# Feed-forward over six PSUM banks, and another deal of the context stream's steps beside the first block

## Chip, cores and metric

The kernel runs on one core of one Trainium2 chip. The metric is device time in microseconds of that core, from one launch that takes all inputs from HBM and writes the output there. A profile of one execution stands beside the timed ones.

## What is computed

Two models run one after the other on 256 tokens of 1024 channels, all in fp32. The first (`first_block`) has two layers, each a hybrid mixer (an SSD branch of 4 groups with 8 heads each, and a retention branch of 4 heads) and a SwiGLU feed-forward. The second (`second_block`) has two layers of latent attention, a Fourier branch and a pooling branch, and after them 128 experts per token, which are rows of two tables picked by top-k. Beside its tokens it carries a context of 256 rows through layer 0, which does not depend on the first model.

```python
def first_block(x, ...):
    for l in range(2):
        h = h + hybrid_mixer(rmsnorm(h, norm_mix_w[l]), ...)
        h = h + swiglu(rmsnorm(h, norm_ffn_w[l]), w_gate_up[l], w_down[l])

def second_block(x, c, ctx, ...):
    for l in range(2):
        last = l == 1
        m_x, m_c = _modulation(c, ...), _modulation(c_ctx, ...)
        hc = _modulate(ctx, norm1_g[l], m_c[0], m_c[1])
        if last: kv_c = _ctx_keys_values(hc, lp)
        else: mix_c, kv_c = _token_mix(hc, lp, None, None)
        mix_x, _ = _token_mix(h, lp, ang, kv_c)
        x = x + m_x[2] * mix_x
        x = x + m_x[5] * _peer(h2, w_pq[l], peer_keys[l], peer_down[l], peer_up[l])
        if not last:
            ctx = ctx + m_c[2] * mix_c
            ctx = ctx + m_c[5] * _peer(hc2, ...)
    return _rmsnorm(x, final_g)
```

`_peer` scores keys, ranks them twice for each of 8 heads, and takes for every token 128 rows of `peer_down` (a dot product with the token) and 128 rows of `peer_up` (a weighted sum).

## The kernel before

The program is a list of items (`put(kind, ...)`); each of the five engines walks the list in its order and does its own part of every item, so the list is the order on PE, DVE (VectorE), ACT (ScalarE), POOL (GpSimd) and SP (SyncE) alike. An engine does what stands next and waits there if its input is not ready.

Two generators make the list. `x_stream` (here the x stream) runs the first model, then the second on x. `context_stream` runs the second model's modulation (48 `mod` items), the context's mixing of layer 0 (attention, Fourier, pooling, gates, `mix`, `token_out`), its queries and ranking, and its experts: 512 steps, each a `fetch` (an indirect DMA of one row for each of 128 tokens, 512 KB, issued by POOL) with a `down` (DVE line 2179) or an `up` (DVE line 2190). The rows come in a ring of nine places.

`streams` deals the two: every `yield` of the x stream adds its number (7 by default) to a clock `ta`, every `yield` of the context stream adds its own to `tb` (1.5 for an expert step), and the context stream moves while `tb <= ta * pace`. `PACES` holds the pace of the modulation, of the mixing, of queries and ranking, and of the experts. When the first model is at its end it yields `"alone"`: what is left of the context stream is put into the list there, ahead of everything that the x stream does in the second model:

```python
            elif step == "alone":
                for _ in live.pop("b", ()):
                    pass
```

A weight chunk is 1 MB, loaded by SP in list order into a ring of slots (three for the mixer of the first model, five for its feed-forward, two for the context). A chunk's products fill one PSUM bank (`Use`, `Banks`), and the bank comes free when DVE or ACT has read it. The mixer uses two banks for chunks (`pa`), two for turns and sums (`pa2`), two for heads and outputs (`py`), and the context two (`pb`). In the feed-forward 22 chunks (`ffn_in`, read by ACT and then by DVE lines 1911 and 1913) go over `wide`, four banks, and then 8 `ffn_out` and 2 `ffn_last` items fill four banks with sums. `ffn_out` number 0 waits until DVE has finished `ffn_in` number 21.

In the SSD branch each of the groups g has `conv_in`, `conv_in`, `gate_in`, `gate_in` of the next group, with four `heads` items between them (PE line 1429 writes the decay logs, ACT lines 2308 to 2314 and DVE lines 1840 and 1841 make the weights, PE lines 1419 to 1421 sum with them), the turn of the group before (`group_end`) and `group_gate`.

## Time and profile before

| | |
|---|---|
| median of 3 runs | 4160.32 us (4160.32 to 4169.17) |
| the profiled execution | 4172.86 us, span of its instructions 4171.6 us |
| PE, DVE, POOL busy | 3669.1 us, 2321.4 us, 1283.5 us |
| DMA | 1208.65 MB, 290 GB/s over the span |

Times in rows count from the first instruction. The profile's L numbers are lines of the kernel before. The first model's two layers take the span's first half, to 2164.8 us, the context stream ends just before that, and the rest is the second model on x. "Idle before" is the time an engine stood still ahead of a group of instructions, and "<-" names what it waited for. PE clk is the granted clock of TensorE as a share of full speed.

### The profile page before, as it was taken

Reading aid. Unit: us, or ns where it says so; the run is one execution under the profiler, and the core shown is the slowest. Engines: PE = TensorE matmul, PEld = TensorE weight load, DVE = VectorE, ACT = ScalarE, POOL = GpSimd, SP = SyncE. Lnnn points to the kernel's source line nnn. Section 1 sums busy time; section 2 is a strip of 40 time slices with the busy share of each in tenths; the row PEclk is TensorE's granted clock in tenths of the full one; section 3 lists DMA queues with packets and bytes.
Section 4 is the critical chain, followed back from the end, with each engine's and each line's share of the span. In section 5 each row is a group of like instructions: output and inputs, shape, how many; then the busy total and the mean of one; then the engine's idle time right before and its main releaser. Section 6 shows DMA issues by size and latency. Waiting matters only on the chain. (4 is left out here: it accounts for less than half of the span.)

```text
span 4171.6 us, 41042 instructions
## 1 busy us (share of the span) xinstructions
PE 3669.1 (88%) x14584; PEld 2587.9 (62%) x14584; DVE 2321.4 (56%) x5464; ACT 657.2 (16%) x1800; POOL 1283.5 (31%) x1125
## 2 busy tenths in 40 slices
PE   8988999998998889999998988777878898877777
PEld 6667788887856778888746874333335786433333
DVE  3432011557767887766751156766763126777875
ACT  2332001110001320100002211111112211111111
POOL 1100000000655566665620013433441002344443
PEclk9999999999999999999999999888999999998889
DMA  8742344334998889998963359988996327999998
GB/s 319 282 194 90 123 151 182 121 129 148 410 396 306 291 327 402 405 383 351 413 250 115 106 223 357 407 344 365 416 414 269 109 106 296 380 420 420 417 419 332
DMA packets 207818, 1208.65 MB, mean 290 GB/s; under 512 B 23696, under 2 KB 24848, under 8 KB 96000
## 3 DMA queue, kind: packets, MB, share of 16 engines
q0 software_dynamic: 154368, 855.71, 51.3%
q1 hardware_dynamic: 53248, 350.32, 22.1%
q8 instruction: 118, 1.93, 0.2%
q14 instruction: 84, 0.69, 0.0%
HBM read 1204.79 MB, written 1.15 MB: 289 GB/s over the span
## 5 line engine op out<-in xcount | busy, mean ns | idle before, releaser
L1308 PE MATMUL bank<-big 128*128 128x256 f32 (+5 forms) x9848 | 2141.4, 378 | 59.8 <-issue 8.7
L1308 PEld LDWEIGHTS bank<-big 128*128 128x128 f32 (+2 forms) x9848 | 1833.9, 191 | 373.6 <-issue 68.0
L2499 POOL DMA_INDIRECT big<-in_pboth,big x1024 | 1219.9, 1191 | 1229.2 <-PE bank L1695 734.8
L1695 PE MATMUL bank<-big 128*128 128x512 f32 x2048 | 1006.0, 650 | 273.5 <-ACT big L2463 273.5
L2179 DVE CUSTOM_DVE_ANT_0 big<-big 128x1024 f32<-128x1024 f32 x768 | 927.5, 1224 | 322.1 <-DMA big<-in_pboth,big 305.4
L1695 PEld LDWEIGHTS bank<-big 128*128 128x128 f32 x2048 | 415.3, 208 | 855.3 <-issue 497.4
L2486 POOL TENSOR_TENSOR big<-big 128x1 f32<-128x1 f32 (+1 forms) x49 | 37.7, 769 | 1502.2 <-DVE big L1749 1502.2
L2190 DVE SCALAR_TENSOR_TENSOR big<-big 128x1024 f32<-128x1024 f32 x254 | 326.3, 1284 | 60.6 <-DMA big<-in_pboth,big 36.6
L2463 ACT ACTIVATE big<-big 128x128 f32<-128x128 f32 x512 | 164.7, 391 | 241.9 <-DVE big L2158 237.0
L1343 PE MATMUL bank<-big 128*128 128x128 f32 x596 | 95.5, 296 | 64.0 <-ACT big L2310 20.6
L2453 ACT ACTIVATE big<-big 128x4 f32<-128x4 f32 (+2 forms) x134 | 27.7, 207 | 725.2 <-DVE big L2154 718.4
L1498 PE MATMUL bank<-big 128*128 128x512 f32 x256 | 114.3, 609 | 19.4 <-DVE big L1913 19.4
L2035 DVE TENSOR_REDUCE big<-bank 128x1 f32<-128x512 f32 (+1 forms) x48 | 28.9, 603 | 173.6 <-PE bank L1596 173.6
L1343 PEld LDWEIGHTS bank<-big 128*128 128x128 f32 x596 | 75.0, 154 | 81.4 <-issue 35.0
L1822 DVE SCALAR_TENSOR_TENSOR big<-big,bank 128x512 f32<-128x512 f32 x32 | 22.0, 688 | 146.2 <-ACT big L2291 143.9
L1498 PEld LDWEIGHTS bank<-big 128*128 128x128 f32 x256 | 49.7, 195 | 83.2 <-issue 63.0
L1899 DVE SCALAR_TENSOR_TENSOR big<-big,bank 128x256 f32<-128x256 f32 x32 | 13.5, 421 | 151.5 <-PE bank L1308 151.4
L1806 DVE SCALAR_TENSOR_TENSOR big<-bank,big 128x255 f32<-128x255 f32 (+1 forms) x144 | 62.7, 478 | 61.6 <-ACT big L2279 59.9
L2248 ACT ACTIVATE big<-big 128x1024 f32<-128x1024 f32 x26 | 27.4, 1055 | 423.8 <-DVE big L1919 160.4
L2057 DVE SCALAR_TENSOR_TENSOR big<-big,bank 128x512 f32<-128x512 f32 x36 | 24.8, 689 | 103.6 <-PE bank L1308 103.6
L2431 ACT ACTIVATE big<-bank,big 128x256 f32<-128x256 f32 x72 | 30.2, 471 | 281.3 <-PE bank L1308 281.3
L2492 POOL DMA_DIRECT2D big<-in_wmod x48 | 25.8, 540 | 152.3 <-PE bank L1520 152.3
(203 smaller groups left out, 2178.5 us busy)
## 6 DMA issues: line engine op xcount, KB each, us to landing
big<-in_w SPq DMA_DIRECT2D x104, 1024.0 KB
big<-in_wmod POOLq DMA_DIRECT2D x48, 1024.0 KB, 8.6
big<-in_wgu SPq DMA_DIRECT2D x44, 1024.0 KB
big<-in_wzg SPq DMA_DIRECT2D x36, 1024.0 KB, 4.8
big<-in_wro SPq DMA_DIRECT2D x32, 1024.0 KB
big<-in_wpq SPq DMA_DIRECT2D x24, 1024.0 KB, 7.0
big<-in_wd SPq DMA_DIRECT2D x22, 1024.0 KB
big<-in_pboth,big POOLq DMA_INDIRECT x1024, 10.1
```

Source lines behind the costliest of these rows:

```text
L1308: last = pe.matmul(o, a, b, start=(i == 0), stop=(i == n - 1))
L1343: last = pe.transpose(o[:, i, :], b, ident)
L1498: last = pe.matmul(us[2 * tt + n].ap, act[:, 2 * i + k, tt * P:tt * P + P], wk[:, k, 512 * n:512 * n + 512], start=(i + k == 0), stop=False)
L1695: last = pe.matmul(u.ap, d.ap, row[:, 512 * i:512 * i + 512], start=(k == 0), stop=(k == 127))
L1806: i = v.scalar_tensor_tensor(c[:, m, s:256], o[:, m, 0:256 - s], conv["w"][m][:, 3 - s:4 - s], c[:, m, s:256], ALU.mult, ALU.add)
L2035: step(v.reduce_max(sm[:, c:c + 1], u.ap[:, 0:nk * P], AX.X))
L2179: v.tensor_tensor_reduce(row, row, h, 1.0, 0.0, ALU.mult, ALU.add, out).then_inc(done[0], 1)
L2190: v.scalar_tensor_tensor(at, s.ap, by, at, ALU.mult, ALU.add).then_inc(done[0], 1)
L2431: last = e.activation(sc.ap[:, m, :], by2(u.ap)[:, m, :], ACT.Tanh, scale=0.5, bias=bias[m])
L2463: s.activation(d.ap, p.ident, ACT.Copy, scale=by).then_inc(diag[0], 1)
L2486: g.tensor_tensor(r.sm[:, 8 + r.at:8 + r.at + r.n], r.sm[:, 4 + r.at:4 + r.at + r.n], r.sm[:, 12:13].to_broadcast([P, r.n]), ALU.pow).then ...
L2499: g.indirect_dma_start(out=s.ap, out_offset=None, in_=table, in_offset=bass.IndirectOffsetOnAxis(ap=index, axis=0)).then_inc(s.full[0], 16)
```

## The change

Five edits, all in the planner. `PACES` of the context: mixing 1.8 to 3.0, queries and ranking 1.1 to 0.9, experts 0.72 to 0.66. Numbers behind `yield` in the SSD branch: in layer 0 of the x stream (`l == 0`) nearly as before, in layer 1 small where DVE has much to do and larger elsewhere. The order inside a group: the turn of the group before stands ahead of a `heads` item instead of behind it, and `dt_sums` and the first `group_mask` come after two of the four first inputs. The last four retention outputs have no context steps between them. The feed-forward has six banks (`six`), and each `ffn_out` waits only for the two activations that it reads.

```diff
@@ -126,7 +126,7 @@
         self.before, self.ss, self.var, self.done = before, ss, var, done
 
 
-PACES = (0.8, 1.8, 1.1, 0.72)
+PACES = (0.8, 3.0, 0.9, 0.66)
 A_SIZE = 27648
 BIG_N = 53208
 SIDE = 8300
@@ -367,7 +367,7 @@
                 w, u = chunk()
                 BC.append(conv(u, 2 * i, qk[:, 2 * i:2 * i + 2, :], None))
                 put("conv_in", ws=[w], hT=hT, conv=BC[i], ready=None if i else hT_ok)
-                yield
+                yield 4 if l else 7
             BC_ok = BC[3]["done"]
             if l == 0:
                 put("block_consts", rmask=rmask, rope=rope)
@@ -514,10 +514,14 @@
                 yield 2
 
             gots = [{"turn": []} for _ in range(8)]
-            yield from group_inputs(0, gots[0])
+            inputs = group_inputs(0, gots[0])
+            for _ in range(2):
+                next(inputs)
+                yield 4 if l else 7
             dts_ok = tick("dt_summed")
             put("dt_sums", u=self.pa2.take(), dts=dts, ready=la_ok, done=dts_ok)
             group_mask(0)
+            yield from inputs
             pairs = group_heads(0, gots[0])
             next(pairs)
             for g in range(4):
@@ -525,13 +529,19 @@
                 end = group_end(g - 1, gots[g - 1]) if g else iter(())
                 for i in range(4):
                     next(nxt)
-                    yield 5.8
+                    if l == 0:
+                        yield 5.8
+                    elif i != 1:
+                        yield 7 if i else 3.5
+                    if i == 1:
+                        next(end, None)
                     next(pairs)
+                    if i == 0:
+                        next(end, None)
                     if i == 2 and g < 3:
                         group_mask(g + 1, gots[g]["cb_read"])
                     if i < 3:
-                        next(end, None)
-                        yield 5.8
+                        yield 6 if i < 2 else 5
                 next(nxt, None)
                 group_gate(g, gots[g])
                 yield 2.5
@@ -568,7 +578,7 @@
                             c.free(self.mt_ok)
                         put("branch_out", ws=[w], u=u, YT=YT, ready=y_ok if n == 0 else [], sig=s.ap[:, m, :], s_ok=s_ok,
                             MT=MT[:, n, :], c=c, done=self.mt_ok)
-                        yield 7.2 if first or n < 6 else 1
+                        yield 7.2 if first or n < 4 else 1
                     s.free(u.free)
 
             yield from merge(True, y_ok, group_end(3, gots[3]))
@@ -609,31 +619,32 @@
             yield 27
 
             fr = Ring([wa[2], wt[0], wt[1], wa[0], wa[1]])
+            six, acts = Banks(self.pa.banks + self.pa2.banks + self.py.banks), []
             for i in range(22):
-                w, u, c = self.load(fr, t["wgu"][l, i], 2048), wide.take(), tmp.take()
+                w, u, c = self.load(fr, t["wgu"][l, i], 2048), six.take(), tmp.take()
                 w.free(u.full)
                 c.free(u.free)
                 put("ffn_in", ws=[w], u=u, hT=hT, c=c, dst=area[:, i, :], tanh=tick("ffn_tanh"),
                     ready=None if i else hT_ok)
-                act_ok = u.free
+                acts.append(u.free)
                 yield
             if l:
                 fw_ok = tick("d_fnorm", 16)
                 put("load_row", dst=fw, src=t["fnorm"][0].to_broadcast([P, 1024]), done=fw_ok, before=[self.x_ok])
-            us = [wide.take() for _ in range(4)]
+            us = [six.take() for _ in range(4)]
             for i in range(8):
                 w = self.load(fr, t["wd"][l, i], 2048)
                 done = tick("ffn_part")
                 w.free(done)
-                put("ffn_out", ws=[w], us=us, act=area, i=i, ready=None if i else act_ok, done=done)
+                put("ffn_out", ws=[w], us=us, act=area, i=i, ready=acts[2 * i + 1], done=done)
                 yield
             ws = [self.load(fr, t["wd"][l, i], 2048) for i in range(8, 11)]
-            put("ffn_last", ws=ws, three=ws, us=us[0:2], act=area, tt=0)
+            put("ffn_last", ws=ws, three=ws, us=us[0:2], act=area, tt=0, ready=acts[17::2])
             put("ffn_add", us=us[0:2], X=X[:, 0, :])
             self.x_ok0 = us[1].free
             r0 = stats(0, late)
             yield 10
-            put("ffn_last", three=ws, us=us[2:4], act=area, tt=1)
+            put("ffn_last", three=ws, us=us[2:4], act=area, tt=1, ready=acts[17::2])
             for w in ws:
                 w.free(us[3].full)
             if l == 0:
@@ -1487,8 +1498,8 @@
 
     def ffn_out(ws, us, act, i, ready, done):
         wk = by2(ws[0].dst)
-        if ready:
-            pe.wait_ge(*ready)
+        pe.wait_ge(*ready)
+        if i == 0:
             for u in us:
                 opened(u)
         pe.wait_ge(*ws[0].full)
@@ -1499,9 +1510,10 @@
                                      start=(i + k == 0), stop=False)
         last.then_inc(done[0], 1)
 
-    def ffn_last(three, us, act, tt, **_):
+    def ffn_last(three, us, act, tt, ready, **_):
         for i, w in enumerate(three):
             wk = by2(w.dst)
+            pe.wait_ge(*ready[i])
             pe.wait_ge(*w.full)
             for k in range(2):
                 for n, u in enumerate(us):
```

In the item list the 512 expert steps are dealt anew. Steps of the context's experts per stretch of the x stream, before and after: feed-forward of layer 0 with its outputs 112 and 103; layer 1 until its first `heads` 31 and 20; its groups up to `branch_gate` 88 and 70; the SSD outputs 44 and 40; retention 78 and 72; retention outputs and `mix_out` 59 and 49; feed-forward with its outputs 100 and 97; behind the last instruction of the first model 0 and 61, of which 4 stand ahead of `"alone"` and 57 are dealt there.

The first place is DVE's queue at the end of the first model. L1919/L1931 is `ffn_add` (before/after), L1924/L1936 `full_norm`, its last work there; L2190/L2202 is `up`, L2209/L2221 and L2212/L2224 `peer_add`, and L1749/L1761 with L1982/L1994 the first norm of the second model. Before:

```order
1835 L2190 SCALAR_TENSOR_TENSOR big<-big 128x1024 x29
1836 L2209 TENSOR_TENSOR big<-big 128x1024 x2
1837 L2212 TENSOR_TENSOR big<-big 128x1024 x2
1838 L1919 SCALAR_TENSOR_TENSOR big<-bank,big 128x512 x2
...
1844 L1924 SCALAR_TENSOR_TENSOR big<-big 128x1024
1845 L1749 TENSOR_SCALAR big<-big 128x1
1846 L1982 TENSOR_SCALAR big<-big 128x1024
```

After:

```order
1820 L2202 SCALAR_TENSOR_TENSOR big<-big 128x1024 x27
1821 L1931 SCALAR_TENSOR_TENSOR big<-bank,big 128x512 x2
...
1828 L1936 SCALAR_TENSOR_TENSOR big<-big 128x1024
1829 L2202 SCALAR_TENSOR_TENSOR big<-big 128x1024 x61
1830 L2221 TENSOR_TENSOR big<-big 128x1024 x2
1831 L2224 TENSOR_TENSOR big<-big 128x1024 x2
1832 L1761 TENSOR_SCALAR big<-big 128x1
1833 L1994 TENSOR_SCALAR big<-big 128x1024
```

The expert steps ended ahead of the first model's last sums; now 61 of them and the context's sum stand between its last instruction and the second model's first.

The second place is DVE's queue in layer 1, group 1, from `heads` to `heads` (L1806/L1818 and L1815/L1827 are `conv_in`, L1862/L1874 the turn of the group before). Before:

```order
1340 L2190 SCALAR_TENSOR_TENSOR big<-big 128x1024 x3
1341 L1840 SCALAR_TENSOR_TENSOR big<-big 128x256
...
1345 L2190 SCALAR_TENSOR_TENSOR big<-big 128x1024 x3
1346 L1806 SCALAR_TENSOR_TENSOR big<-bank,big 128x255 x2
...
1349 L1815 SCALAR_TENSOR_TENSOR big<-big 128x512
1350 L2190 SCALAR_TENSOR_TENSOR big<-big 128x1024 x3
1351 L1840 SCALAR_TENSOR_TENSOR big<-big 128x256
...
1355 L1862 TENSOR_TENSOR big<-bank,big 128x4x128 x2
```

After:

```order
1287 L2202 SCALAR_TENSOR_TENSOR big<-big 128x1024
1288 L1852 SCALAR_TENSOR_TENSOR big<-big 128x256
...
1292 L2202 SCALAR_TENSOR_TENSOR big<-big 128x1024 x3
1293 L1818 SCALAR_TENSOR_TENSOR big<-bank,big 128x255 x2
...
1296 L1827 SCALAR_TENSOR_TENSOR big<-big 128x512
1297 L1874 TENSOR_TENSOR big<-bank,big 128x4x128 x2
1298 L1852 SCALAR_TENSOR_TENSOR big<-big 128x256
```

No expert step stands any more between a `conv_in` and the `heads` behind it, and one instead of three ahead of the first `heads`.

The third place is SP's queue where the context goes from its mixing to its queries, in layer 0. `in_iota` and `in_keys` wait for the context's last `token_out` (the load of `in_wout` is its weight); `in_w` and `in_wro` are chunks of the x stream. Before:

```order
76 L2517 DMA big<-in_wout 128x2048 x3
77 L2517 DMA big<-in_w 128x2048
78 L2562 DMA big<-in_iota 128x16
79 L2566 DMA big<-in_keys 128x2048
80 L2517 DMA big<-in_w 128x2048 x2
```

After:

```order
66 L2529 DMA big<-in_wout 128x2048 x2
67 L2574 DMA big<-in_iota 128x16
68 L2578 DMA big<-in_keys 128x2048
69 L2529 DMA big<-in_wro 128x2048
```

A chunk of the x stream stood between the last weight and the wait; now the next chunk of the x stream is behind it.

## Rows read from the trace of the kernel before

**Rows 1.** The page: busy time, share of the span and instructions of each engine.

```profile
PE 3669.1 (88%) x14584; PEld 2587.9 (62%) x14584; DVE 2321.4 (56%) x5464; ACT 657.2 (16%) x1800; POOL 1283.5 (31%) x1125
```

**Rows 2.** Stretches of the first model: start and end, length, busy times, clock, DMA.

```profile
core 0: us, PE busy (x) PEld busy (x) DVE busy (x) ACT busy (x) POOL busy (x), PEclk, DMA share, GB/s
...
857.30:1009.50 152.20, 140.89 (x651) 120.61 (x649) 105.82 (x398) 12.61 (x24) 1.82 (x3) 0.98 0.37 132
1009.50:1182.00 172.50, 154.79 (x704) 134.19 (x705) 125.79 (x281) 8.54 (x23) 100.42 (x80) 0.96 0.90 358
...
1269.10:1396.20 127.10, 110.42 (x527) 96.62 (x527) 105.63 (x189) 27.68 (x71) 67.43 (x52) 0.89 0.83 300
1396.20:1547.00 150.80, 125.86 (x675) 110.89 (x674) 133.87 (x183) 50.71 (x142) 91.02 (x71) 0.92 0.87 318
1547.00:1790.20 243.20, 238.86 (x1101) 205.27 (x1101) 181.17 (x288) 18.38 (x39) 163.10 (x128) 0.99 1.01 401
1790.20:1924.20 134.00, 125.93 (x572) 106.37 (x570) 74.03 (x121) 10.22 (x18) 69.03 (x54) 0.97 0.93 360
1924.20:2087.20 163.00, 152.76 (x704) 132.99 (x704) 122.90 (x129) 8.45 (x22) 112.92 (x84) 0.98 0.99 398
```

**Rows 3.** DVE in order of time, end of the first model: start, length, line, idle before.

```profile
2086.90 16.89 DVE L2190 SCALAR_TENSOR_TENSOR big<-big 128x1024 f32<-128x1024 f32 x12
...
2136.84 2.36 DVE L2209 TENSOR_TENSOR big<-big 128x1024 f32<-128x1024 f32 x2 [4.74 <-DMA big<-mods]
2139.24 2.36 DVE L2212 TENSOR_TENSOR big<-big 128x1024 f32<-128x1024 f32 x2
...
2167.72 1.29 DVE L1924 SCALAR_TENSOR_TENSOR big<-big 128x1024 f32<-128x1024 f32 x1 [0.74 <-POOL big L2486]
2171.49 0.15 DVE L1749 TENSOR_SCALAR big<-big 128x1 f32<-128x1 f32 x1 [2.49 <-DMA big<-in_cs]
```

**Rows 4.** PE in order of time: the second model's first chunk.

```profile
2176.88 7.43 PE L1308 MATMUL bank<-big 128*128 128x128 f32 x35 [1.74 <-DVE big L1989]
```

**Rows 5.** PE in order of time, both feed-forwards: three idle spells.

```profile
1046.11 10.23 PE L1308 MATMUL bank<-big 128*128 128x256 f32 x38 [8.55 <-DVE big L1913]
...
1182.01 2.90 PE L1498 MATMUL bank<-big 128*128 128x512 f32 x3 [9.12 <-DVE big L1913]
...
2087.24 10.99 PE L1498 MATMUL bank<-big 128*128 128x512 f32 x21 [10.28 <-DVE big L1913]
```

**Rows 6.** DVE in order of time: the first expert step.

```profile
1044.03 1.23 DVE L2179 CUSTOM_DVE_ANT_0 big<-big 128x1024 f32<-128x1024 f32 x1 [8.12 <-DMA big<-in_pboth,big]
```

**Rows 7.** PE in order of time: the first mix_out of layer 0.

```profile
970.37 4.89 PE L1308 MATMUL bank<-big 128*128 128x256 f32 x12 [5.36 <-issue]
```

**Rows 8.** PE's waits, 1396.2 to 1547 us: line, for whom, us, times, longest.

```profile
PE bank L1343 <- ACT big L2310: 15.2, 3, 6.6
PE bank L1419 <- DVE big L1841: 9.8, 5, 2.7
```

**Rows 9.** Groups of DVE instructions, 1396.2 to 1547 us: busy us, mean ns.

```profile
L2190 DVE SCALAR_TENSOR_TENSOR big<-big 128x1024 f32<-128x1024 f32 x67 | 86.0, 1284 | 5.9 <-issue 0.4
```

**Rows 10.** SP, then PE, in order of time: the modulation's end.

```profile
272.02 1.14 SPq L2540 DMA_DIRECT2D mods<-big  x4
274.20 0.36 SPq L2517 DMA_DIRECT2D big<-in_w  x1
...
272.13 1.09 PE L1343 MATMUL bank<-big 128*128 128x128 f32 x4 [3.18 <-DVE big L1942]
...
282.45 1.94 PE L1343 MATMUL bank<-big 128*128 128x128 f32 x8 [4.96 <-ACT big L2265]
```

**Rows 11.** SP, then PE, in order of time: the context's last token_out.

```profile
704.95 0.91 SPq L2517 DMA_DIRECT2D big<-in_w  x2
...
712.05 4.14 PE L1308 MATMUL bank<-big 128*128 128x256 f32 x11 [2.56 <-DMA big<-in_w]
```

**Rows 12.** PE in order of time, the context's mixing: an attention step, a gate.

```profile
381.35 0.41 PE L1343 MATMUL bank<-big 128*128 128x128 f32 x2 [1.13 <-ACT big L2412]
...
492.92 67.35 PE L1308 MATMUL bank<-big 128*128 128x256 f32 x302 [2.93 <-DMA big<-in_wzg]
```

## Prediction

> **What bounds the kernel now.** I read the page's busy shares first, then the stretches, then the idle spells of PE and DVE inside them. PE is busy for 3669 of 4171.6 us [rows 1], so the end moves only where PE gains or loses idle time or clock. By stretches [rows 2] the first model has three regimes. In the SSD outputs and the retention (1547 to 1790 us) PE is busy for 238.9 of 243.2 us: nothing to gain. In the feed-forwards PE misses 17.7 of 172.5 us and 10.2 of 163.0, nearly all of it in spells of 8.55, 9.12 and 10.28 us that wait for DVE [rows 5]. In layer 1 from 1269 to 1547 us PE is busy for 236 of 278 us at a clock of 0.89 and 0.92, while DVE is busy for 240: DVE's expert steps set the pace there. The context stream ends just ahead of the second model, so a step dealt earlier costs or saves nothing by itself; a step left at the end would have DVE alone.
>
> **The bill at the end.** 61 `up` steps now stand on DVE between `full_norm` and the second model's first norm, which feeds PE's first chunk. Twelve in a run took 16.89 us, 1.41 each [rows 3]: 61 x 1.41 = 85.8 us. Behind them the wait of `peer_add` for the modulation's row (4.74) and its two instructions (2 x 2.36) make 9.5 [rows 3], and the first chunk follows the norm by 2176.88 - 2171.49 = 5.4 [rows 3, 4]. Today the whole way from the end of `full_norm` (2169.0) to that chunk is 7.9. So the end pays 85.8 + 9.5 + 5.4 - 7.9 = **92.8**. Bounds: at 1.284 a step, the mean among other work [rows 9], the steps take 78.3, and if the row of the modulation is there early 4.7 go: 80.6. If each step took a tenth more: 101. A fetch moves 0.524 MB; at 401 GB/s [rows 2] that is 1.31 us, so DMA doesn't make it longer than DVE.
>
> **What the first model gives back.**
> - Feed-forward of layer 0. The 8.55 us come when a chunk finds none of four banks free, since DVE reached its `ffn_in` behind the ranking and a first expert step that waited 8.12 for its rows [rows 6]; six banks let PE run two chunks (some 14 us) further. The 9.12 come because `ffn_out` 0 waits for activation 21, now for activation 1. The same matmuls take 152.8 busy in layer 1 and 154.8 here at the lower clock; I take 153.8, so 172.5 becomes 153.8: **-18.7**, and about 2 (that difference of clock) behind the second spell: **-2.1**.
> - The end of layer 0's mixer (857 to 1009.5): 11.3 idle, 5.36 of it ahead of the first `mix_out` [rows 2, 7]. With no context steps between the last four outputs DVE makes that input early, and fewer ranks stand there: **-8.3**; bounds 0 and 11.3.
> - Layer 1 until group 1 (127.1 us, DVE 105.6): 50 steps become 35, that is 31 to 20 and 19 to 15. 15 steps at 1.33, about midway between 1.284 and 1.41, are **-20**. PE's 110.4 at 0.89 are about 100 at full clock, so the floor is not met.
> - Groups 1 to 3 (150.8, DVE 133.9, 67 steps [rows 9]): 12 fewer x 1.284 = 15.4. PE waits 15.2 us for ACT's line 2310 and 9.8 for DVE's 1841 [rows 8]; the first has other causes (the order of ACT), so I take **-12**. Bounds: 0, and PE alone at full clock, 125.9 x 0.92 = 116 to 118, a gain of 33.
> - 1547 to 1790: 4.3 idle [rows 2], **-3**. Then to 1924: 8.1 idle, with ten steps fewer **-2**, since the norm's chain stands there in any case.
> - Feed-forward of layer 1: the spell of 10.28 and its clock, **-11**.
>
> Together **-77.1**.
>
> **A rule against the move.** In layer 1 from 1547 us on the steps now lie under PE work: PE 98%, DVE 74%, DMA 1.01 [rows 2]; before that DVE was the limit. The Trainium skill ("Perfetto Trace Analysis", Optimization Strategy) says that a kernel with several regimes may gain by interleaving them; the change does the reverse for the steps at the end. This case's trace agrees for the retention and not for the groups. By the rule alone (rival E) the time would be 4239, by the rows 4194.
>
> **What layer 0 loses by the faster mixing.** Mixing steps move ahead of where they stood, so PE meets more of them in a row, each with a chain of its own.
> - The modulation's end: PE waits 3.18 and 4.96 there [rows 10], with x chunks between. SP's store of the modulation (272.02) had an x chunk's load behind it; now the load of the values' weight stands behind that wait, and `low_rank` directly behind the turn that feeds it: one more such wait, the mean of a longer one and clock, **+5.8** (bounds 0 and 9).
> - Attention: a step right behind another waited 1.13 for ACT [rows 12]; four or five more of them in runs, and two more in keys and values: **+7**. Against that the gate's load wait of 2.93 and its clock go, as the gates now stand further apart from the load of their first weight: **-4.1** [rows 12]. Bounds of the two together: -4 and +12.
> - The end of the mixing: `in_iota` and `in_keys` wait on SP for the last `token_out`. An x chunk's load stood ahead of them and the chunk's wait was 2.56 [rows 11]; now the next x chunk is queued behind. From issue to use was 712.05 - 704.95 = 7.1; with the two loads of keys ahead about 9.4, so +6.8, and 2.2 of clock: **+9** (bounds 0 and 12).
>
> Together **+17.7**.
>
> **Sum.** 92.8 - 77.1 + 17.7 = +33.4. The profiled execution has a span of 4171.6 (its time 4172.9), 12 above the median of the runs, 4160.3, which is the lowest of them too; the difference carries to the median: 4160.3 + 33.4 = **4194**. The measurement can tell about 0.3%, 12.5 us, from no change.
>
> **Rivals.**
> - A, the forecast, own range 4178 to 4208 (the bill's bounds are -12 and +8, those of layer 0's losses -22 and +6, and they don't all fall together): **0.49**.
> - B, payback in full and no new waits: in layer 0 the mixing steps hide behind x chunks (17.7 back), groups 1 to 3 give 15.4 and not 12, and retention's end 7 and not 2: 4194 - 17.7 - 8.4 = 4168, with bounds 4160 to 4173. For it: the losses rest on queue order, of which no row shows the new form. Against: the SP queue's wait is certain, only its length isn't. **0.20**.
> - C, the other side, faster: layer 1's groups and inputs become bound by PE alone. Then 277.9 falls to 100 + 117 = 217, a gain of 61 in place of 32, and with B's layer 0: 4194 - 29 - 17.7 = 4147. It decides once the gains less losses pass 92.8 + 12.5 = 105. For it: DVE's load falls by a fifth there and six yields move steps away from `heads`. Against: PE's 15.2 us for ACT don't depend on them. **0.11**.
> - D, the feed-forward keeps its length: its DMA share is 0.90 and 0.99 (358 and 398 GB/s [rows 2]), so with PE's spells gone the chunks come late instead. About 30 of the 18.7 + 2.1 + 11 is missing: 4194 + 30 = 4224. Against: layer 0 has room for 401 GB/s, 172.5 x 358/401 = 154, and both have fewer fetches. Half of it, in layer 1, gives 4204, still A. **0.15** for over 4208.
> - E, no step that is taken out of layer 1 or the mixer's end gives anything back, since PE would wait there for ACT or its own sums: 20 + 12 + 8.3 + 3 + 2 = 45 are missing, 4239. For it: the 15.2 us for ACT [rows 8]. Against: DVE's 133.9 of 150.8 and 105.6 of 127.1 us, with PE below full clock because it stands still. **0.05**.
>
> **Numbers.** The range from 4163 to 4221 takes in A, most of B and over half of D. Faster by over 0.3% is C, 0.11; within 0.3% is B, 0.20; slower is A, D and E, 0.69.
>
> **What would show it.** In the profile after: PE idle for about 105 us between `ffn_last` and the first chunk of the second model (12 today: 2164.8 to 2176.9), DVE's line 2202 x61 at 1.41 each, and line 2221 behind it with a wait for `mods` of about 5. No spell of 8 to 10 us in either feed-forward. Layer 1 to the end of group 3 some 246 us in place of 278. The first model's last PE work near 2165 - 59 = 2106. In layer 0 an idle spell of about 9 us that ends with the load of an `in_wro` chunk after the last `token_out`, and a wait of PE for the values' weight at the modulation's end. Wrong would make it: steps at the end at 1.28 or less or a modulation's row that is loaded ahead (toward B), PE bound groups (C), a DMA share at 1.0 in the feed-forwards with PE waiting for `wgu` or `wd` (D).

## The result, and the profile after

The changed kernel takes 4233.36 us (median of 4 runs, 4227.09 to 4244.06), beside 4163.78 us for the kernel before on the same chip: the ratio is 1.0167, with a 95% interval of 1.0145 to 1.0188. It is slower by some 70 us, where +33 was forecast, and lies above the range.

The page of the changed kernel, busy times; it answers to [rows 1]:

```profile
PE 3648.2 (86%) x14584; PEld 2573.9 (61%) x14584; DVE 2324.1 (55%) x5464; ACT 658.4 (16%) x1800; POOL 1284.0 (30%) x1125
```

The stretches of the changed kernel, cut at the same places of the program as those of [rows 2]. The first one is all up to the first feed-forward, the last two are the way from the matmuls that stand behind the first model's last sums to the second model's first chunk, and the second model from there on:

```profile
core 0: us, PE busy (x) PEld busy (x) DVE busy (x) ACT busy (x) POOL busy (x), PEclk, DMA share, GB/s
0.00:1036.00 1036.00, 947.17 (x4684) 771.46 (x4684) 360.50 (x1073) 175.49 (x441) 37.38 (x70) 0.96 0.46 171
1036.00:1188.60 152.60, 152.59 (x704) 133.22 (x705) 104.65 (x215) 8.26 (x22) 89.92 (x74) 1.00 0.94 378
1275.30:1382.90 107.60, 100.92 (x526) 88.73 (x527) 84.85 (x182) 28.11 (x71) 45.07 (x37) 1.00 0.80 279
1382.90:1527.10 144.20, 124.05 (x674) 110.81 (x674) 117.86 (x170) 50.81 (x142) 72.50 (x57) 0.93 0.77 281
1527.10:1772.80 245.70, 238.75 (x1101) 205.19 (x1101) 173.53 (x230) 18.29 (x39) 149.09 (x119) 0.99 0.98 380
1772.80:1903.10 130.30, 123.32 (x572) 105.29 (x570) 61.02 (x113) 10.03 (x17) 57.12 (x45) 1.00 0.86 328
1903.10:2055.70 152.60, 152.60 (x704) 133.19 (x705) 111.80 (x166) 8.26 (x22) 101.01 (x77) 1.00 0.98 394
...
2133.50:2238.40 104.90, 9.25 (x36) 7.31 (x37) 88.59 (x78) 6.35 (x13) 61.25 (x55) 0.54 0.87 322
2238.40:4225.80 1987.40, 1639.82 (x5202) 945.71 (x5202) 1130.96 (x3125) 345.13 (x1021) 584.95 (x527) 0.94 0.77 311
```

Read from the top, this is the account, forecast first. Up to the first feed-forward +17.7 - 8.3 = +9.4, measured 1036.0 - 1009.5 = **+26.5**. First feed-forward 172.5 to 152.6, forecast -18.7, measured -19.9; what stands behind it -2.1 and -0.4. Layer 1 until group 1: -20 and -19.5. Groups 1 to 3: -12 and **-6.6**. Until 1790 us: -3 and **+2.5**. The mixer's end: -2 and -3.7. Last feed-forward with its outputs: -11 and -12.3. So the first model's last sums end 33.4 us earlier (2164.9 to 2131.5). The matmuls behind them wait for `ffn_add`, which in the changed kernel stands behind expert steps:

```profile
2133.48 6.27 PE L1364 MATMUL bank<-big 128*128 128x256 f32 x20 [1.94 <-DVE big L1931]
```

The forecast counts the bill from the end of DVE's `full_norm`. That comes 31.6 us earlier (2169.0 to 2137.4), not 59.4, and from there to the second model's first chunk it is 101.0 us instead of 7.9: +93.1, where 92.8 was forecast. The first chunk comes 2238.4 - 2176.9 = 61.5 us later. From there on the program is the same in both kernels, and took 1994.7 us in the profile before and 1987.4 in this one.

### The profile page after: what moved, and what is told of

Its sections match the earlier page's. It is cut to its first block and busy times, and to the rows that moved or that the text cites. A ratio compares the mean times of both kernels' runs of the same rounds, so it can differ in the third digit from the quotient of the medians.

```text
span 4225.8 us, 41067 instructions
## 1 busy us (share of the span) xinstructions
PE 3648.2 (86%) x14584; PEld 2573.9 (61%) x14584; DVE 2324.1 (55%) x5464; ACT 658.4 (16%) x1800; POOL 1284.0 (30%) x1125
## 5 line engine op out<-in xcount | busy, mean ns | idle before, releaser
L1319 PE MATMUL bank<-big 128*128 128x256 f32 (+4 forms) x9848 | 2134.2, 377 | 50.4 <-DMA big<-in_wro 9.5
L1319 PEld LDWEIGHTS bank<-big 128*128 128x128 f32 (+1 forms) x9848 | 1828.0, 191 | 361.4 <-issue 72.5
L2202 DVE SCALAR_TENSOR_TENSOR big<-big 128x1024 f32<-128x1024 f32 x254 | 326.4, 1285 | 40.8 <-DMA big<-in_pboth,big 15.7
L1354 PEld LDWEIGHTS bank<-big 128*128 128x128 f32 x596 | 73.8, 153 | 172.5 <-issue 139.3
L1818 DVE SCALAR_TENSOR_TENSOR big<-bank,big 128x255 f32<-128x255 f32 (+1 forms) x144 | 62.7, 477 | 62.4 <-ACT big L2291 60.7
```

What stands on the lines that cost most here:

```text
L1319: last = pe.matmul(o, a, b, start=(i == 0), stop=(i == n - 1))
L1354: last = pe.transpose(o[:, i, :], b, ident)
L1818: i = v.scalar_tensor_tensor(c[:, m, s:256], o[:, m, 0:256 - s], conv["w"][m][:, 3 - s:4 - s], c[:, m, s:256], ALU.mult, ALU.add)
L2202: v.scalar_tensor_tensor(at, s.ap, by, at, ALU.mult, ALU.add).then_inc(done[0], 1)
```

## Experiments

Each ratio below is that of the kernel's runs to those of the kernel before on the same chip. "First chunk" is the start of the second model's first chunk in the profile (2176.9 before, 2238.4 in the changed kernel), "first feed-forward" the start of that stretch (1009.5 and 1036.0). Both are free of what the second model itself varies by, but not of all chance: in the kernel before, with six banks alone and in the two kernels with half of a step's work or bytes, DVE's queue is the same up to the first feed-forward, and that begins at 1009.5, 1011.7, 1006.1 and 1011.2. A difference of up to 5 or 6 us in it is no finding from one profile each.

### One part alone: six banks

The kernel before with this part of the change (and what `ffn_last` needs for it):

```diff
+            six, acts = Banks(self.pa.banks + self.pa2.banks + self.py.banks), []
-                w, u, c = self.load(fr, t["wgu"][l, i], 2048), wide.take(), tmp.take()
+                w, u, c = self.load(fr, t["wgu"][l, i], 2048), six.take(), tmp.take()
-                put("ffn_out", ws=[w], us=us, act=area, i=i, ready=None if i else act_ok, done=done)
+                put("ffn_out", ws=[w], us=us, act=area, i=i, ready=acts[2 * i + 1], done=done)
```

> The kernel before with one part of the change: six banks and the waits on single activations; the deal and the order in the groups stay. Theory 1 (the parts add up, and this one is worth what the two feed-forwards gained in the changed kernel, 20.5 + 10.3 us): no spell of 8 us or more in either feed-forward, the second model's first chunk at 2176.9 - 31 = 2146 us, time 4133 us. Rival (part of the gain needs the lighter deal, because with 111 and 100 steps beside them DVE falls further behind than six banks cover): spells of 3 to 6 us stay and the time is 4145 to 4155 us.

It took 4159.31 us, ratio 0.9969 (0.9959 to 0.9980), some 13 us less than before; the first chunk at 2165.7. PE in order of time, in both feed-forwards:

```profile
1175.05 5.12 PE L1499 MATMUL bank<-big 128*128 128x512 f32 x7 [10.60 <-DVE big L1915]
...
2130.83 4.67 PE L1510 MATMUL bank<-big 128*128 128x512 f32 x6 [9.53 <-DMA big<-in_wd]
```

The spell of 8.55 us is gone, those of 9.12 and 10.28 us are not: one still waits for DVE, 10.60 us long, at the first `ffn_out`; the other now stands at `ffn_last` and waits for a weight. Two more banks let PE run ahead by a few chunks, and then it stands before the same late work. Nor is it so that `ffn_out` number 0 "waits only for the two activations that it reads": its four banks of sums come out of the six too, and are those of `ffn_in` 16 to 19 (counted from 0), so that it waits for activation 19 where it waited for 21. DVE finishes number 19 here, and 0.25 us later PE starts:

```profile
1174.38 0.42 DVE L1915 TENSOR_TENSOR big<-big,bank 128x256 f32<-128x256 f32 x1
```

In the five other runs with six banks in which PE waits over 1 us at the first `ffn_out` of layer 0, it starts within 0.3 us of the same activation. The rival was right in kind, and its spells are longer still than it said.

### One part alone: the paces

```diff
-PACES = (0.8, 1.8, 1.1, 0.72)
+PACES = (0.8, 3.0, 0.9, 0.66)
```

> The kernel before with the new paces and nothing else: 29 steps stand behind the last sums instead of 66, 28 and 81 steps in layer 1's inputs and groups. Theory 1 (layer 0 pays for the paces what it paid in the changed kernel, 18 to 26 us; the end 24 x 1.41 + 7 = 41 us; a step taken out of the first model gives about 1 us back): 4164 + 22 + 41 - 28 = 4199 us. Rival (without six banks and the new order the steps taken out give nothing, because the waits that they stand behind remain): 4225 us or more.

4207.54 us, ratio 1.0098 (1.0081 to 1.0115), some 42 us more; first chunk 2215.9. PE's wait at the end, and the stretches of the mixer's end of layer 0 (its last 572 matmuls; the row in [rows 2] has 651) and of both feed-forwards:

```profile
2212.24 1.94 PE L1343 MATMUL bank<-big 128*128 128x128 f32 x8 [42.98 <-DVE big L1982]
```

```profile
890.30:1045.00 154.70, 130.53 (x572) 109.82 (x570) 98.56 (x364) 10.66 (x19) 11.66 (x13) 0.92 0.42 155
1045.00:1199.40 154.40, 152.79 (x704) 133.03 (x704) 108.55 (x199) 8.47 (x22) 97.89 (x77) 1.00 1.00 401
...
1930.80:2085.50 154.70, 152.78 (x704) 133.05 (x705) 114.02 (x131) 8.79 (x23) 100.42 (x76) 1.00 1.00 399
```

With four banks and the wait on activation 21, both feed-forwards take 154.4 and 154.7 us: the lighter deal (102 and 93 steps there, before 111 and 100) does alone what I had put down to the banks. The order of the groups is the old one here, and PE's waits in groups 1 to 3 are still those of [rows 8], somewhat shorter:

```profile
PE bank L1343 <- ACT big L2310: 11.4, 3, 5.2
PE bank L1419 <- DVE big L1841: 9.0, 4, 3.7
```

Ahead of the feed-forwards stands the loss: the first feed-forward begins at 1045.0, 35.5 us late, more than the 22 us of the expectation. Its total of 4199 came near only because the feed-forwards paid back what I had not counted.

### The mixing's and the ranking's paces set back

The changed kernel with

```diff
-PACES = (0.8, 3.0, 0.9, 0.66)
+PACES = (0.8, 1.8, 1.1, 0.66)
```

> The changed kernel with the paces of mixing and of queries and ranking set back to 1.8 and 1.1 (experts stay at 0.66). Theory 1 (layer 0 loses its 26.5 us by these two paces alone): the first feed-forward begins at 1009 to 1012 us again, not at 1036; 9 more steps stand at the end, 9 x 1.41 = 13 us, so the second model's first chunk comes at 2238.4 - 26.5 + 13 = 2225 us and the time is 4220 us. Rival (the reordered group and its yields in layer 0 cause part of it): the feed-forward begins at 1020 or later, and the time is 4232 us or more.

4213.03 us, ratio 1.0100 (1.0080 to 1.0120); first chunk at 2226.2, 1.2 us from the number given. The first feed-forward begins at 1006.2, and the stretch that ends there was as in the first row; the second is PE's wait ahead of the second model:

```profile
861.60:1006.20 144.60, 138.54 (x653) 119.28 (x651) 82.42 (x307) 12.67 (x25) 1.83 (x3) 1.00 0.38 138
```

```profile
2222.50 1.94 PE L1354 MATMUL bank<-big 128*128 128x128 f32 x8 [107.20 <-DVE big L1994]
```

PE is idle for 6.1 of 144.6 us there, before for 11.3 of 152.2 [rows 2]. So the mixer's end gains the 7 to 8 us of the forecast (the last version below, where the empty outputs stand without the other edits, has some 7), and the two paces cost layer 0 29.8 us (1036.0 - 1006.2): 20.1 of it are idle time of PE, the rest is clock, and of that up to 5 or 6 us can be chance. With mixing back at 1.8, the wait for the values' weight at the modulation's end is still there:

```profile
285.97 8.78 PE L1319 MATMUL bank<-big 128*128 128x256 f32 x32 [6.11 <-DMA big<-in_w]
```

With the paces alone (mixing at 3.0, old order) it is not: PE waits 3.18, 4.97, 0.81 and 1.74 us in that place, much as before. So the new order and its yields make it, and not the faster mixing.

### The ranking's pace alone set back

```diff
-PACES = (0.8, 3.0, 0.9, 0.66)
+PACES = (0.8, 3.0, 1.1, 0.66)
```

> The changed kernel with the pace of queries and ranking alone set back to 1.1 (mixing stays at 3.0, experts at 0.66). Behind the first model 42 steps stand instead of 66 (5 of them ahead of the last norm in both), and 24 steps go ahead of the first feed-forward. Theory 1 (of layer 0's 26.5 us, some 11 come from the slower ranking, whose steps stand ahead of score_v in the retention, and the rest from the mixing's pace): the spell of 7.43 us goes, the first feed-forward begins at 1025 to 1028 us, the end has 24 x 1.41 = 34 us less, time 4233 - 34 - 8 + 5 = 4196 us. Rival (mixing at 3.0 makes all of the loss, since it moves the ranking wherever it is paced): the feed-forward begins at 1036 us or later, time 4205 us or more.

4208.26 us, ratio 1.0100 (1.0083 to 1.0117). The first feed-forward begins at 1050.4: later than in the changed kernel, so theory 1 falls and the rival stands. PE in order of time, layer 0's retention:

```profile
920.82 2.05 PE L1469 MATMUL bank<-big 128*128 128x512 f32 x2 [10.80 <-DVE big L1893]
```

with 5.47 and 6.01 us for line 1903 ahead of it and behind it, and the same place of the changed kernel:

```profile
907.73 2.05 PE L1469 MATMUL bank<-big 128*128 128x512 f32 x2 [7.43 <-DVE big L1893]
...
923.85 1.94 PE L1354 MATMUL bank<-big 128*128 128x128 f32 x8 [3.91 <-DVE big L1903]
```

Lines 1893 and 1903 are DVE's part of `scores` and `head_gate`, short work that stands behind ranking steps. The slower ranking had made these waits shorter. In layer 0 of the kernel before PE never waits for these two lines, and with mixing at 1.8 and ranking at 1.1 the longest such wait is 1.01 us. It takes the mixing at 3.0 to bring the ranking among the retention's heads, or a faster ranking: with mixing at 1.8, ranking at 1.3 and 1.5 (below) waits 5.02 and 11.48 us at line 1903.

### The order of one load

The changed kernel with one more yield where the context goes from mixing to queries:

```diff
         yield "pace", PACES[2]
+        yield 7
```

> The changed kernel with one more yield of 7 between the context's mixing and its queries, so that the x stream's next chunk is loaded ahead of the loads that wait for the last token_out; one ranking head goes behind. Theory 1 (the 9.47 us spell is SP's queue order alone): the spell falls to 2 to 3 us, the first feed-forward begins 8 to 10 us earlier, time 4224 us. Rival (the load was late for its slot of the ring anyway, or the time comes back as a spell at the next wait of layer 0): within 3 us of the changed kernel's 4233 us.

4230.47 us, ratio 1.0140 (1.0123 to 1.0157), against 1.0167 (1.0145 to 1.0188): the intervals overlap. The changed kernel had

```profile
664.52 10.03 PE L1319 MATMUL bank<-big 128*128 128x256 f32 x32 [9.47 <-DMA big<-in_wro]
```

and here PE runs through:

```profile
637.74 38.30 PE L1320 MATMUL bank<-big 128*128 128x256 f32 x176
```

The spell was SP's queue order, as the prediction has it. The first feed-forward begins at 1029.4, 6.6 us earlier, and by the end of the first model this is gone: the last sums end at 2131.2 here and at 2131.5 in the changed kernel. What took it back is in layer 1, groups 1 to 3, above all; the stretch here, to be held against 144.20 of the changed kernel:

```profile
1378.00:1526.40 148.40, 130.09 (x674) 116.14 (x674) 117.95 (x170) 50.82 (x142) 73.40 (x57) 0.90 0.76 273
```

DVE has the same work (117.95 and 117.86), the matmuls are the same 674, but they are busy for 130.09 and not 124.05 us at a clock of 0.90 and not 0.93. The rival's return of the time is what happened, by the clock and not by a new wait. With one profile of each I can't say how often it falls so.

### No steps behind the first model

```diff
-PACES = (0.8, 3.0, 0.9, 0.66)
+PACES = (0.8, 3.0, 0.9, 0.76)
```

> The changed kernel with the experts' pace at 0.76 in place of 0.66: no step is left behind the first model; its layer 0 feed-forward takes 118 steps and not 103, layer 1 up to the groups' end 104 and not 90. Theory 1 (a step at the end costs 1.41 us, one in layer 1's inputs and groups about 1.3 us, one elsewhere nothing): 93 us less at the end, 14 x 1.3 = 18 us more in layer 1, so 4233 - 93 + 18 = 4158 us. Rival (the steps cost the same wherever they stand, DVE being the limit in all of the first model): 61 x 1.3 = 79 us more there, 4220 us.

4199.00 us, ratio 1.0072 (1.0053 to 1.0090); first chunk 2204.0, 34.4 us earlier than in the changed kernel, where theory 1 had 75 and the rival 13. Neither holds. The bill is gone, but `full_norm` ends at 2196.5 instead of 2137.4: 61 steps put back go with 59.0 us, 0.97 each, and not in layer 1's groups alone. 5.2 of the 59.0 us were there at the first feed-forward (1041.2 and 1036.0), up to which DVE's queue is the same in both, so they are chance; from there on it is 53.8 us, 0.88 a step. The last feed-forward, PE in order of time:

```profile
2103.37 58.11 PE L1509 MATMUL bank<-big 128*128 128x512 f32 x128 [5.49 <-DVE big L1925]
2169.07 23.29 PE L1520 MATMUL bank<-big 128*128 128x512 f32 x48 [7.58 <-DMA big<-in_wd]
```

### What limits the steps: half of DVE's work, half of the rows

Two kernels on the kernel before. The first halves what DVE does in a step (half of each row is left out of the sums):

```diff
         v.wait_ge(*full)
+        if half:
+            row, h = row[:, 0:512], h[:, 0:512]
```

and the same in `up`.

> The kernel before, where each of the context's down and up steps works on 512 of 1024 channels (half of the row is left out; the first up of each half of the tokens is whole); rows are fetched whole. It takes DVE's work and leaves the DMA's. Theory 1 (in the feed-forwards, the outputs and the retention the rows' arrival sets the pace, at a DMA share of about 1.0, and DVE's own work only in layer 1's inputs and groups): the spells of 9.12 and 10.28 us at the feed-forwards' ends stay over 5 us each, layer 1 from 1269 to 1547 shrinks from 278 to 235 to 245 us, time about 4125 us. Rival (DVE's work is the limit in all of them): the spells go as well, 4100 us or less.

The second halves what a fetch brings:

```diff
-        g.indirect_dma_start(out=s.ap, out_offset=None, in_=table,
+        out, src = (s.ap[:, 512 * half - 512:512 * half] if half else s.ap), table
+        g.indirect_dma_start(out=out, out_offset=None, in_=src,
```

> The kernel before, where each of the context's fetches from the tenth on brings 512 of 1024 channels of a row of another place (half of the rows' bytes are left out, and the sums are of other values); DVE does all its work. Theory 1 (the rows' arrival sets the feed-forwards' spells): 8.55, 9.12 and 10.28 us go or fall below 4 us, layer 1's inputs and groups stay within 10 us of 278, time 4164 - 28 = 4136 us. Rival (DVE's own work is behind the spells): they stay over 6 us each, 4160 us.

Half of DVE's work gives 4117.02 us, ratio 0.9876 (0.9860 to 0.9893); half of the rows 4140.93 us, ratio 0.9934 (0.9918 to 0.9951). Layer 1's inputs and its groups, then the last feed-forward, with half of DVE's work:

```profile
1263.10:1373.30 110.20, 103.83 (x527) 91.24 (x527) 78.90 (x190) 27.91 (x71) 55.75 (x52) 0.97 0.89 335
1373.30:1505.50 132.20, 121.40 (x675) 107.89 (x674) 98.52 (x182) 50.76 (x142) 78.88 (x71) 0.96 0.97 369
1877.50:2038.50 161.00, 152.84 (x705) 133.11 (x705) 79.22 (x128) 8.45 (x22) 81.56 (x84) 0.98 1.00 399
```

and with half of the rows:

```profile
1263.60:1391.40 127.80, 109.69 (x526) 96.05 (x527) 105.79 (x190) 27.72 (x71) 67.99 (x52) 0.89 0.60 195
1391.40:1538.40 147.00, 125.63 (x674) 111.29 (x674) 133.33 (x183) 50.78 (x142) 90.28 (x71) 0.93 0.63 207
1915.40:2070.10 154.70, 152.80 (x704) 133.03 (x704) 124.15 (x129) 8.48 (x22) 108.10 (x84) 1.00 0.83 288
```

The two stretches of layer 1 take 242.4 us with half of DVE's work and 274.8 with half of the rows, 277.9 before: they are DVE's. The last feed-forward is the other way round, 161.0 and 154.7, 163.0 before: with DVE's work cut from 122.9 to 79.2 us its spell is still 8.15 us, and with fewer bytes it falls to 1.92 (PE in order of time, the one and the other):

```profile
2038.46 6.73 PE L1498 MATMUL bank<-big 128*128 128x512 f32 x9 [8.15 <-DVE big L1913]
```

```profile
2070.15 5.40 PE L1498 MATMUL bank<-big 128*128 128x512 f32 x12 [1.92 <-DVE big L1913]
```

Its wait is named as one for DVE, but DVE is late there because its rows are, at a DMA share of 1.00. DVE's own waits in the last feed-forward of the kernel before (us, times, longest) say so too:

```profile
DVE big L2190 <- DMA big<-in_pboth,big: 31.6, 30, 2.5
```

In layer 0's feed-forward both count: its spell of 9.12 us at the first `ffn_out` becomes 6.25 with half of the work and 1.67 with half of the rows. Layer 0's spell behind the first steps, 8.55 before (9.08 us with half of the rows, 8.21 with half of the work), answers to neither. Behind it stand the ranking and the first rows' latency, as the prediction has it; no run takes these two apart. Theory 1 holds in the first kernel, and in the second but for this spell, which it had going.

### Versions with the parts that looked good

All four have six banks and leave no step to be dealt at `"alone"`; they differ in paces and in order.

With the new order and paces 1.8, 1.1, 0.76:

> The changed kernel with mixing and ranking paces of before (1.8, 1.1) and the experts at 0.76, so that nothing is left at the end: six banks, single waits and the new order in the groups stay. Theory 1 (parts add up): feed-forwards -31 us, layer 1's inputs and groups with 104 steps in place of 119 about -18 us, layer 0's mixing as before: 4164 - 49 = 4115 us. Rival (in the groups only the smaller number of steps counted, and what is dealt elsewhere comes back as waits in retention and outputs): 4130 us or more.

4171.83 us, ratio 1.0002 (0.9992 to 1.0011): nothing, where 4115 was expected, and above the rival's 4130 by far. Its first feed-forward and its end, PE in order of time:

```profile
1170.20 5.33 PE L1509 MATMUL bank<-big 128*128 128x512 f32 x7 [16.52 <-DVE big L1925]
...
2170.85 1.94 PE L1354 MATMUL bank<-big 128*128 128x128 f32 x8 [13.11 <-DVE big L1994]
```

The first feed-forward begins 8.6 us earlier than before and waits for 16.5; nine steps still stand behind the last sums, and PE waits 13.1 there. With paces 1.8, 1.3, 0.76:

> As the kernel with paces 1.8, 1.1 and 0.76, with the ranking at 1.3: the ranking ends ahead of the first feed-forward, no step is left behind the last sums (there 9), and the first feed-forward has 118 steps in place of 108. Theory 1 (the 16.5 us spell there came from DVE with two ranking heads and the late start of the steps, and the 13.1 us ahead of the second model from the nine late steps): both spells fall below 6 us, and the time is 4150 us. Rival (DMA is full from the first fetch on, so the later stages wait as much as those two gain): 4165 us or more.

4181.75 us, ratio 1.0031 (1.0019 to 1.0042). With 1.8, 1.5, 0.74:

> Six banks, single waits and the new order of the changed kernel, with the paces 1.8 for mixing, 1.5 for ranking and 0.74 for the experts: 18 steps go ahead of the first feed-forward, 115 and 98 into the two feed-forwards with what stands around them, 79 into the groups, none behind the first model. Theory 1 (rows' arrival limits the first model from the first fetch on, so the way to gain is to begin the fetches earlier; nothing is left at the end): the second model's first chunk at about 2155 us, time 4150 us. Rival (ranking at 1.5 stands ahead of the retention's score_v as in the run with mixing at 3.0 and ranking at 1.1, and costs 10 to 20 us there, all that the earlier fetches give): 4165 us or more.

4180.44 us, ratio 1.0022 (1.0012 to 1.0032). In both the ranking is ahead of the feed-forward and cuts into the retention and its outputs instead, and the first feed-forward begins at 1028.3 and 1039.2; PE in order of time in the latter:

```profile
983.15 2.08 PE L1319 MATMUL bank<-big 128*128 128x256 f32 x4 [11.89 <-DVE big L1911]
```

Both rivals' times held. The reason that the first of them gave, a full DMA, is not what the trace shows first: the two spells that were to fall did fall (to 3.73 and 0.79 us), and the loss stands ahead of the feed-forward. The last version is the kernel before with six banks, the empty last outputs and the experts at 0.74:

> The kernel before with six banks, single waits, no context steps between the last four outputs, and the experts at 0.74 in place of 0.72 so that none is left behind the last sums. Theory 1 (the empty outputs alone take the spell of 5.36 us and its clock out of layer 0's end, as in the run with mixing set back, about 7 us): the first feed-forward begins at about 1004 us, its idle spell grows by less than that, and the time is 4152 us. Rival (what PE gains ahead of the first feed-forward it waits for inside it, because ranking and rows end no earlier): the feed-forward's spell grows from 10.6 to 15 us or more, and the time is within 4 us of the kernel with six banks alone, 4159 us.

4159.45 us, ratio 0.9987 (0.9978 to 0.9996). The first feed-forward begins at 1003.8 instead of 1011.7 (six banks alone; part of that may be chance), and PE waits ahead of its first `ffn_out`

```profile
1172.55 7.87 PE L1499 MATMUL bank<-big 128*128 128x512 f32 x12 [15.93 <-DVE big L1915]
```

which is 5.3 us longer. The rival held again. Six banks alone, at 0.9969, is the best version that I have.

## Why the prediction was wrong

The sign and the largest term held. At the first chunk the sum was 28 us short (+33.4 forecast, +61.5 measured), of which layer 0 is 17 and layer 1 eleven, 5.4 of it in the groups and 5.5 behind them. Two more steps of the forecast failed without showing in its sum: what six banks do for the feed-forwards, and where the wait at the modulation's end comes from.

**The bill at the end was right.** DVE in order of time, the changed kernel; it answers to [rows 3]:

```profile
2136.13 1.31 DVE L1936 SCALAR_TENSOR_TENSOR big<-big 128x1024 f32<-128x1024 f32 x1 [0.74 <-POOL big L2498]
2137.36 46.68 DVE L2202 SCALAR_TENSOR_TENSOR big<-big 128x1024 f32<-128x1024 f32 x33
2184.53 39.60 DVE L2202 SCALAR_TENSOR_TENSOR big<-big 128x1024 f32<-128x1024 f32 x28 [0.49 <-DVE big L2202]
2228.22 2.36 DVE L2221 TENSOR_TENSOR big<-big 128x1024 f32<-128x1024 f32 x2 [4.08 <-DMA big<-mods]
```

61 steps in 86.3 us, 1.41 each (85.8 forecast), and 4.08 for the modulation's row (4.74).

**The term that failed most is layer 0's, +17.7 - 8.3: +9.4 forecast, +26.5 measured.** Its parts in the changed kernel, PE in order of time from the modulation's end to the keys; the first rows answer to [rows 10]:

```profile
278.00 1.09 PE L1354 MATMUL bank<-big 128*128 128x128 f32 x4 [6.44 <-DVE big L1954]
285.04 8.65 PE L1319 MATMUL bank<-big 128*128 128x256 f32 x32 [5.95 <-DMA big<-in_w]
295.57 1.07 PE L1354 MATMUL bank<-big 128*128 128x128 f32 x8 [1.87 <-ACT big L2277]
297.86 1.60 PE L1354 MATMUL bank<-big 128*128 128x128 f32 x8 [1.22 <-ACT big L2376]
301.19 9.27 PE L1319 MATMUL bank<-big 128*128 128x128 f32 x48 [1.73 <-DVE big L2001]
```

The values' weight behind the stored modulation is there, 5.95 us; with the row ahead of it and three turns behind, these are 17.2 us of idle time where I had +5.8 over the 8.1 of before. But I put that term under "what layer 0 loses by the faster mixing", and the run with mixing set back has the same wait while the one with the paces alone has not: the size was near by luck, the cause is the new order with its yields. The 9.47 us behind `token_out` are there too (9 forecast for all of it). What I had not seen at all is the ranking ahead of `scores` and `head_gate`: 7.43 + 3.91 us. I counted ranking steps for each stretch (7 and 6 in the mixer's end) and took fewer for better; what counts is which short DVE step they stand ahead of. So the -8.3 of the empty outputs, which the run with mixing set back shows to be real, was turned into a loss: from 800 us to the first feed-forward PE is idle for 11.5 us before and 16.2 in the changed kernel. That is the step that failed, a term for ranking steps ahead of short DVE work that I had put at nothing. Up to the first feed-forward PE's idle time is 1036.0 - 947.2 = 88.8 us, before

```profile
0.00:1009.50 1009.50, 938.93 (x4684) 768.21 (x4684) 347.70 (x1023) 174.94 (x441) 37.31 (x70) 0.97 0.47 175
```

70.6: 18.3 of the 26.5 us are idle time, and 8.2 are as many matmuls (4684 in both rows) at a lower clock. The forecast names 2.2 us of clock in one term and nothing for the rest; identical queues differ by 5 to 6 us there, so part of the 8.2 is chance.

**Layer 1's groups, -12 forecast, -6.6 measured.** PE's waits there in the changed kernel; they answer to [rows 8]:

```profile
PE bank L1440 <- DVE big L1874: 11.0, 2, 6.9
PE bank L1430 <- DVE big L1853: 9.1, 3, 3.8
```

The 15.2 us for ACT's line 2310 are gone, and in their place PE's line 1440 waits 11.0 us for DVE's line 1874. That line is the turn of the group before, `group_turn`, which the new order put ahead of `heads`: the third edit of the diff, which I had costed at nothing. The paces alone, in the old order, have 11.4 + 9.0 us here, and the changed kernel has 11.0 + 9.1: one wait took the other's place. No run has the new order alone. The -6.6 is itself uncertain by some 4 us of clock: the kernel with the chunk's load first, the same in this stretch, took 148.4 us, which would be -2.4. From 1527 us on, 245.7 us in place of 243.2, I had taken 3 of 4.3 idle us as a gain, and idle time is 6.9 there. It is one wait, the one that was 4.3 us before, at the start of the SSD outputs, now longer:

```profile
1541.23 1.94 PE L1354 MATMUL bank<-big 128*128 128x128 f32 x8 [6.95 <-ACT big L2277]
```

**The feed-forwards, -31.8 forecast, -32.6 measured up to the last sums, for another reason.** They came out right in the changed kernel, but six banks alone keep spells of 10.60 and 9.53 us, and the paces alone, without six banks, bring both to 154 to 155 us. Two steps failed. "The 9.12 come because `ffn_out` 0 waits for activation 21, now for activation 1" is wrong as to what it waits for now: its banks of sums hold it until activation 19, as the run with six banks shows. And a lag of DVE was read as one that two banks cover: DVE is late because rows are, and the row that says so is the DMA share of 0.99 and 0.90 in [rows 2]. That the sum of these terms came out was luck: the lighter deal had made DVE's lag go, not the banks. Rival D had that mechanism, and gave it the wrong condition. It decides when the deal is as dense as before (the runs with six banks alone, at 0.76, and the last one), not in the changed kernel, whose deal is lighter.

**The rule against the move.** The page "Perfetto Trace Analysis" of the Trainium skill (Optimization Strategy) says that a kernel with several regimes may gain by interleaving them. The trace agrees in part. The runs at 0.76 and 0.66 put a price on it: a step at the end costs 1.41 us, and taking it out of the first model gives back 0.97 (59.0 / 61) with mixing at 3.0, and 0.64 with mixing at 1.8, where `full_norm` ends at 2111.9 with 66 more steps behind it than in the version where it ends at 2154.4 (42.4 / 66). Each pair has the same DVE queue up to the first feed-forward and differs by 5 us there, in opposite directions; counted from that place the two are 0.88 (53.8 / 61) and 0.72 (47.7 / 66). Not nothing, as rival E had it, and never the full price, as B and C needed.

**The median.** The first chunk is 61.5 us late, the medians are 69.6 apart, and the two profiled spans 54.2. I carried the profile's own sum to the median as if both were exact. The profiled execution before was 9.1 us above its median of 4163.8, that of the changed kernel 6.3 below its own, which is the whole of 69.6 - 54.2; and the median that I added to, 4160.3, had become 4163.8 with the fourth run. The second model, the same program in all these kernels, took from 1985 to 1998 us in the fourteen profiles of this study, so a span holds that much chance in either direction; the 8 us between 61.5 and 69.6 are of that size, and I have no other cause for them.

## What to carry to other kernels

Work dealt beside a stream costs by what the stream lacks at that place, DVE or DMA, and a wait "for DVE" doesn't tell which: look at the DMA share beside it, and at what DVE itself waits for. A deeper buffer moves such a wait a few chunks on and removes it only when the late work catches up; put the number of steps that are due by then against it. When a dealer's pace is changed, list what now stands directly ahead of each short step that PE waits for, and count the work left at the end first: its price of 1.41 us a step was in the trace of before, and over the whole first model a step taken out gave back 0.7 to 0.9. When a ring of banks is made longer, look at who takes the next places of it: here the sums did, and kept the wait for all but two of the activations.

## What was not expected of the hardware

The same instructions took a different time in stretches that no edit touches, with the clock as the only difference. Layer 0's stretch from `branch_gate` to the retention, in the profile before and in the kernel with half of the rows, whose first fetch comes 490 us later:

```profile
354.30:543.20 188.90, 170.26 (x791) 143.27 (x790) 25.56 (x70) 27.83 (x83) 0.69 (x1) 0.96 0.31 112
```

```profile
351.00:545.00 194.00, 175.45 (x792) 147.06 (x792) 25.58 (x71) 27.89 (x83) 0.69 (x1) 0.93 0.30 109
```

The idle time is the same 18.6 us; the granted clock was 0.96 and 0.93 (of full speed, 2.4 GHz; it falls to 1.2 GHz), and PE was busy for 5.2 us more. The busy times of the other engines agree within 0.1 us. A term for "the clock behind a spell" is then an average, and a gain of 6 us, as in the kernel with the chunk's load first, can vanish in it. The same shows at the first feed-forward: with the same DVE queue up to there it began at 1036.0 and 1041.2 us (experts at 0.66 and 0.76, mixing at 3.0), and at 1006.2 and 1000.9 (mixing at 1.8).
